# Shared up blocks inside the expert sweep, extra units between expert 61 and expert 62

## The reference

```python
scores = jax.nn.sigmoid(xs @ router_w)                 # 512 x 64
_, idx = lax.top_k(jnp.where(emask, sel, -jnp.inf), 6) # 6 experts of 64 per token
w = w / jnp.sum(w, axis=-1, keepdims=True) * 2.5
# every chosen (token, expert) pair: (silu(x @ w1[e]) * (x @ w3[e])) @ w2[e], width 256
routed = jax.ops.segment_sum(yg, slot_tok)             # summed per token with weight w
return routed + swiglu(xs, sh_w1, sh_w3, sh_w2)        # plus one shared expert, width 256
```

## Time and profile before

| | |
|---|---|
| median of three runs | 2140.44 us |
| profiled execution | 2133.77 us, of which the span is 2131.8 us |
| mean granted PE clock | 0.948 |
| PE busy | 1854.0 us (87%) |
| DVE busy | 859.0 us (40%) |
| ACT busy | 461.1 us (22%) |
| POOL busy | 373.6 us (18%) |
| SP's DMA queue | 499.70 MB, 58.3% of the time of the 16 engines |
| chain that ended last | PE 57%, DMA 19%, DVE 10%, issue 5%, POOL 5%, ACT 3% |

### The profile page before, as it was taken

How to read it: one execution, slowest core, us unless ns; L and a number is a source line. 1 busy time by engine, 2 the same in 40 slices (tenths; PEclk the granted TensorE clock), 3 DMA queues, 4 the chain that set the end, 5 groups by cost and what they waited for, 6 DMA issues and landing times.

```text
span 2131.8 us, 30544 instructions
## 1 busy us (share of the span) xinstructions
PE 1854.0 (87%) x9472; PEld 966.6 (45%) x9473; DVE 859.0 (40%) x1527; ACT 461.1 (22%) x823; POOL 373.6 (18%) x563
## 2 busy tenths in 40 slices
PE   5989999885999888788998899876889899989996
PEld 3455555333544444444444443344444444444543
DVE  1546666556322222222115499566222221212226
ACT  4134444212101011111110565220111111101112
POOL 0010000001111111111105288002111111111113
PEclk9999999996999999999999999887999999999997
DMA  9488010347999999999997202256999999999955
GB/s 405 176 340 330 1 40 20 139 173 304 357 420 393 402 400 394 401 404 396 383 382 262 123 1 119 79 227 269 399 406 402 399 387 408 402 400 396 398 182 211
DMA packets 95680, 625.10 MB, mean 293 GB/s; under 512 B 16128, under 2 KB 16256, under 8 KB 57472
## 3 DMA queue, kind: packets, MB, share of 16 engines
q1 hardware_dynamic: 44640, 499.70, 58.3%
q0 software_dynamic: 26112, 79.72, 10.3%
q10 hardware_dynamic: 24864, 44.84, 5.8%
HBM read 563.38 MB, written 76.28 MB: 300 GB/s over the span
## 4 chain that ended last, share of the span: by engine, by line
PE 57%; DMA 19%; DVE 10%; issue 5%; POOL 5%; ACT 3%; SPq 0%; POOLq 0%; DVEq 0%; ACTq 0%
DMA ring<-in 18%; PE PS L1064 12%; PE PS L1058 9%; PE PS L1071 6%; PE PS L1096 4%; PE PS L1085 4%; PE PS L1286 3%; PE PS L1049 3%; PE PS L986 3%; POOL work L581 3%; POOL work L613 3%; PE PS L1040 2%; PE PS L949 2%; PE PS L1004 2%; PE PS L1014 2%
## 5 line engine op out<-in xcount | busy, mean ns | idle before, releaser
L1064 PE MATMUL PS<-ring,work 128*64 128x256 f32 x3360 | 419.6, 406 | 112.8 <-issue 110.2
L1064 PEld LDWEIGHTS PS<-ring,work 128*64 128x64 f32 x3360 | 248.0, 146 | 260.5 <-issue 165.6
L1457 DVE TENSOR_TENSOR work<-work,PS 64x256 f32<-64x256 f32 x105 | 44.4, 423 | 521.9 <-ACT work L666 520.0
L1071 PE MATMUL PS<-ring,work 128*64 128x512 f32 x840 | 203.3, 605 | 1.0 <-DVE work L1469 1.0
L1058 PE MATMUL PS<-ring,work 128*128 128x512 f32 x400 | 184.3, 615 | 19.9 <-issue 8.6
L533 POOL COPY col_i<-idx 128x1 int32 (+1 forms) x128 | 23.4, 182 | 793.2 <-PE PS L1096 785.8
L1463 DVE COPY work<-PS 128x1024 f32<-128x1024 f32 x128 | 156.7, 1225 | 13.6 <-PE PS L1096 9.7
L539 POOL DMA_INDIRECT work<-h_rows,col_i x128 | 124.9, 976 | 165.2 <-issue 165.2
L666 ACT ACTIVATE work<-PS 64x256 f32<-64x256 f32 x105 | 39.5, 376 | 519.1 <-PE PS L1064 516.7
L1096 PE MATMUL PS<-cst,work 128*128 128x128 f32 x1040 | 142.4, 281 | 9.9 <-DMA work<-h_rows,col_i 9.9
L1096 PEld LDWEIGHTS PS<-cst,work 128*128 128x128 f32 x1040 | 115.0, 142 | 62.9 <-issue 52.8
(11 more groups left out here) (247 smaller groups left out, 2176.9 us busy)
## 6 DMA issues: line engine op xcount, KB each, us to landing
ring<-in SPq DMA_DIRECT2D x156, 2048.0 KB, 8.6
ring<-in SPq DMA_DIRECT2D x132, 1024.0 KB, 11.0
y_rows<-sq POOLq DMA_DIRECT2D x2, 14336.0 KB, 58.0
y_rows<-work ACTq DMA_DIRECT2D x210, 128.0 KB
ring<-in SPq DMA_DIRECT2D x3, 4096.0 KB, 15.4
y_rows<-work ACTq DMA_DIRECT2D x46, 256.0 KB
ring<-in SPq DMA_DIRECT2D x2, 3072.0 KB, 16.8
work<-in SPq DMA_DIRECT2D x2, 2048.0 KB, 17.4
```

What stands on the lines that cost most here:

```text
L1064: last = mm(bank(6)[64 * q:64 * q + 64, 0:F], lhs(c)[:, 0:64], w13(s)[:, q, c, :], start=(c == 0), stop=(c == DC - 1), tile_position=(0, 6 ...
L1071: last = mm(bank(4)[64 * q:64 * q + 64, :], actT[par][:, kk, 0:64], w2(s)[:, kk, q * 512:(q + 1) * 512], start=(kk == 0), stop=(kk == 1), ...
```

## The change

- The shared up weights go into `acc` (free between the row stores and the combine), at the start of SP's refills, with `sh_in`. Only the shared down weights still use a ring slot, now slot 2, after expert 61's down product.
- The loop over experts 3 to 62 becomes four loops (`PARTS`: experts 3 to 18, 19 to 30, 31 to 46, 47 to 58), on PE, DVE and ACT. After each PE makes one shared up block, and after the second and fourth ACT and DVE work it off. Experts 59 to 63 are written out.
- The extra units run between `unit(61)` and `unit(62)`. They have buffers of their own (`unit_x`, `unit_xT`, `unit_gate`, `unit_act`, `unit_actT`, `unit_y`), which lie in `acc` over the shared up weights, used up by then. Their weights go into slot 0.
- Expert 62 now uses slot 1 and expert 63 slot 3, so they follow experts 59 and 60 there. SP issues the extra unit's weights before theirs.
- Before expert 61's down product PE waits for expert 62's gate.
- The pointwise weights after layer 0 go out one expert earlier: the first DMA behind expert 61's down product, the second behind expert 62's.

```diff
+        shared_w13 = acc.rearrange("p t d -> p (t d)").rearrange("p (a c f) -> p a c f", a=2, c=DC)
+        unit_x, unit_xT, unit_y = acc[:, 0, :], acc[:, 1, :].rearrange("p (c t) -> p c t", c=DC), acc[:, 3, :]
+        unit_gate, unit_act, unit_actT = acc[:, 2, 0:F], acc[:, 2, F:2 * F], acc[:, 2, 2 * F:3 * F].rearrange("p (k t) -> p k t", k=2)
-        SHARED, EXTRA = 3, 2
+        SHARED, EXTRA = 2, 0
+        PARTS = ((0, 4), (4, 7), (7, 11), (11, 14))
         def slot_of(u):
-            return (3, 2, 0, 1)[u % RING]
+            return {E - 2: 1, E - 1: 3}[u] if u >= E - 2 else (3, 2, 0, 1)[u % RING]
...
# SP
+                sp.dma_start(acc.rearrange("p t d -> p (t d)"), sh_w[i][:, 0:UP]).then_inc(sh_in, 16)
                 refill_up(4, slot_of(4))
...
-                sp.wait_ge(m["up_ps"], E - 3)
-                sp.dma_start(slot_ap(SHARED)[:, 0:UP], sh_w[i][:, 0:UP]).then_inc(sh_in, 16)
-                refill_down(E - 1, slot_of(E - 1))
-                sp.wait_ge(m["dn_ps"], E - 3)
-                sp.dma_start(slot_ap(SHARED)[:, UP:SLOT], sh_w[i][:, UP:SLOT]).then_inc(sh_in, 16)
+                refill_up(E - 3, slot_of(E - 3))
+                refill_down(E - 4, slot_of(E - 4))
+                refill_down(E - 3, slot_of(E - 3))
                 sp.wait_ge(unit_rdy, i + 1)
-                sp.wait_ge(m["dn_ps"], E - 2)
+                sp.wait_ge(m["dn_ps"], E - 5)
...              (the loop over the extra units' weights)
+                sp.wait_ge(m["up_ps"], E - 4)
+                expert_up(ds(E - 2, 1), slot_of(E - 2), w_in[slot_of(E - 2)])
+                sp.wait_ge(m["dn_ps"], E - 4)
+                expert_down(ds(E - 2, 1), slot_of(E - 2), w_in[slot_of(E - 2)])
...              (the same for E - 1, one later)
+                sp.wait_ge(m["dn_ps"], E - 2)
+                sp.dma_start(slot_ap(SHARED)[:, UP:SLOT], sh_w[i][:, UP:SLOT]).then_inc(sh_in, 16)
...
+            load_pw1(0, 3)
             sp.wait_ge(M[0]["dn_ps"], E - 1)
-            load_pw1(0, 3)
-            sp.wait_ge(M[0]["dn_ps"], E)
             load_pw1(3, 6)
# PE
+                pe.wait_ge(sh_in, 16 + 32 * i)
+                for part, (g0, g1) in enumerate(PARTS):
+                    with nc.tensor.Fori(0, g1 - g0) as g:
+                        for r in range(4):
+                            unit(g * 4 + (4 * g0 + 3 + r), ...)
+                    if part == 2:
+                        pe.wait_ge(sh_gate, 1 + 2 * i)
+                    elif part == 3:
+                        pe.wait_ge(sh_act, 1 + 2 * i)
+                    shared_up(part // 2, part % 2)
+                for u in range(E - 5, E - 2):
+                    unit(u, slot_of(u), slot_of(u - 1), 32 * loads_of(u), 16 * ((u + 1) // 2 + 1), u % 2)
+                many = nc.tensor.value_load(unit_i[0:1, XMAX:XMAX + 1], min_val=0, max_val=XMAX)
+                with nc.tensor.If(many > 0):
+                    pe.wait_ge(xgT_ev, E - 1 + i * E)
+                    with nc.tensor.Fori(0, many) as j:
+                        ...      (the extra unit's four steps, with unit_x, unit_xT, unit_act, unit_actT)
+                unit(E - 2, ..., 0, E - 1 + i * E)      # with the wait for the gate
                 unit(E - 1, slot_of(E - 1), slot_of(E - 2), 32 * loads_of(E - 1), None, 1)
                 either(E - 1, lambda big: down(E - 1, 1, slot_of(E - 1), big))
# POOL: the extra unit's gather stands between those of expert 62 and expert 63
```

More of the change, by code:

```diff
@@ L549, in moe @@
                 gather(1, 1, xg_in[1])
-                with nc.gpsimd.Fori(0, E // 2 - 1) as g:
+                with nc.gpsimd.Fori(0, E // 2 - 2) as g:
                     for r in range(2):
@@ L705, in moe @@
                 either(1, lambda big: store(1, 0, 1, big))
[L706 to L713, removed]
                 def shared_silu(blk):
@@ L1172, in expert_in, with unit @@
                     pe.wait_ge(xgT_ev, u + 1 + i * E)
-                    pe.wait_ge(w_in[slot], n_w + i * 32 * LOADS)
+                    pe.wait_ge(w_in[slot], n_w + i * 32 * LOADS[slot])
                     either(u, lambda big: up(u, lambda c: xgT[par][:, c, :], slot, big))
-                def unit(u, slot, below, n_w, n_next, par):
+                def unit(u, slot, below, n_w, n_next, par, gates=None):
                     expert_in(u, slot, n_w, par)
@@ L1179, in unit @@
                         turn_rows(u + 1, n_next, 1 - par)
+                    if gates is not None:
+                        pe.wait_ge(gate_rdy, gates)
                     if below is not None:
@@ L1194, in moe, with shared_up @@
                 unit(2, slot_of(2), slot_of(1), 32, 32, 0)
-                with nc.tensor.Fori(0, (E - 4) // 4) as g:
-                    for r in range(4):
-                        unit(g * 4 + (3 + r), slot_of(3 + r), slot_of(2 + r), g * 32 + 32 * loads_of(3 + r),
-                             g * 32 + 16 * ((4 + r) // 2 + 1), (1 + r) % 2)
+                def shared_up(blk, a):
+                    for c in range(DC):
+                        last = mm(bank(3 * a), shared_w13[:, a, c, blk * 128:blk * 128 + 128], hM[:, c, :], start=(c == 0), stop=(c == DC - 1))
+                    last.then_inc(sh_ps, 1)
@@ new lines, in moe @@
+                pe.wait_ge(sh_in, 16 + 32 * i)
+                for part, (g0, g1) in enumerate(PARTS):
+                    with nc.tensor.Fori(0, g1 - g0) as g:
+                        for r in range(4):
+                            unit(g * 4 + (4 * g0 + 3 + r), slot_of(3 + r), slot_of(2 + r), g * 32 + (32 * g0 + 32 * loads_of(3 + r)),
+                                 g * 32 + (32 * g0 + 16 * ((4 + r) // 2 + 1)), (1 + r) % 2)
+                    if part == 2:
[3 more added lines that the diff above has]
+                    shared_up(part // 2, part % 2)
@@ L1200, in moe @@
+                unit(E - 2, slot_of(E - 2), slot_of(E - 3), 32 * loads_of(E - 2), 16 * ((E - 1) // 2 + 1), 0, E - 1 + i * E)
                 unit(E - 1, slot_of(E - 1), slot_of(E - 2), 32 * loads_of(E - 1), None, 1)
                 either(E - 1, lambda big: down(E - 1, 1, slot_of(E - 1), big))
-                def shared_up(blk, a):
-                    for c in range(DC):
-                        last = mm(bank(3 * a), w13(SHARED)[:, a, c, blk * 128:blk * 128 + 128], hM[:, c, :], start=(c == 0), stop=(c == DC - 1))
-                    last.then_inc(sh_ps, 1)
```

156 lines of the change are left out of this document (86 added, 70 removed).

## The result

The changed kernel takes 2159.16 us, the median of four runs (2157.22 to 2161.67), against 2140.07 us (2138.6 to 2141.09, also four runs) for the kernel before: ratio 1.0103, 95% interval 1.0087 to 1.0120, so 19.1 us slower. The forecast was 2155.4 us, slower.

The account below looks back on a forecast made before the run. Weight loads bound part of each sweep, PE its end. Terms summed to +8.7 us (layer 0) and +6.3 (layer 1), +15.0 together: 2148.8 us on the profiled execution, 2155.4 us as median, own range 2149 to 2162.

Parts of the forecast that it names:

- shared up weights at the start: Sweep start: 2 MB load slows first row gathers, 1.5 us (layer 0) and 3 (layer 1), upper bounds 2.5 and 4.7.
- blocks 1 to 3: After experts 18, 30, 46, mostly where loads lead: cost 0 in layer 0 (at most 1.5 us), 2 us in layer 1.
- block 4: After expert 58, where PE has no spare time: costs 7.1 us in layer 0, 6.6 in layer 1.
- extra unit: Between experts 61 and 62: 15.1 us serial chain plus 1.5 for count, branch and loop exit, 16.6 us per layer.
- end to first gather: Last down product to first combine gather: 26.3 us before, now 9.8 in layer 0 and 4.4 in layer 1.
- What bounds the kernel: Loads set the pace in some stretches of the sweep; at both sweeps' ends PE does, so work added there costs nearly full length.
- Rival A: Sweep's end: loads set the pace after all, fourth block and extra unit vanish there; 2108 us, faster, 7%.
- the sign that the prediction named for C: Behind expert 30: a DMA share below 1 in the following 20 us would show that loads run dry.
- rival C's first half: Loads run dry behind expert 30 in layer 1 (+5.1 us) and in layer 0 (+1.5); whole rival 2165 us, 15%.
- Rival D: Sweep's end: four loops and written-out experts cost PE idle time, 4.2 us per layer; 2164 us, 13%.
- the case in which it must wait for the loads: Layer 0's last store stuck until loads drain: gap of 12 us, sum 2.2 us higher.
- the rule quoted in the prediction: Layer 0's last store: DMA engines take turns between queues, so loads slow it but it need not wait until they drain.

Follow-up runs that it names:

- e10: Changed kernel with expert 63's result copied into a free piece of acc, not the buffer expert 61's store holds: 2157.87 us, 1.0098 to the kernel before.
- e3: Changed kernel with the four shared up blocks after experts 22, 26, 46 and 50, not 18, 30, 46 and 58: 2141.07 us, 1.0013 to the kernel before.
- e1: Changed kernel with the first two pointwise loads after layer 0 held until all expert stores have landed: 2160.07 us, 1.0108 to the kernel before.
- e5: Kernel before with only the shared up blocks moved, after experts 18, 30, 46 and 58; extra unit still behind expert 63: 2151.46 us, 1.0066.
- e4: Changed kernel with the shared blocks back behind the sweep under the gathers, so only the extra unit is moved: 2135.35 us, 0.9989 to the kernel before.
- e11: Kernel with only the extra unit moved, plus expert 63's result copied into a piece of acc: 2137.53 us, 1.0001 to the kernel before.
- e2: Changed kernel with the shared up weights issued behind the first refill, not ahead of it: 2155.09 us, 1.0079 to the kernel before.
- e7: Changed kernel with blocks after experts 22, 26, 46 and 50 and shared up weights behind the first refill: 2139.97 us, 1.0005 to the kernel before.
- e6: Kernel before with blocks after experts 22, 26, 46, 50, shared up weights behind the first refill, extra unit behind the sweep: 2137.75 us, 0.9995.

## Why the prediction was right, step by step

In the profiled pair, with e10 as a second execution of the same sweep; both in us.

| step | forecast L0 / L1 | changed kernel L0 / L1 | e10 L0 / L1 |
|---|---|---|---|
| shared up weights at the start | 1.5 / 3 | 2.9 / 6.5 | 1.4 / 6.7 |
| blocks 1 to 3 | 0 / 2 | 3.4 / 5.5 | -0.4 / 6.2 |
| block 4 | 7.1 / 6.6 | 6.9 / 6.4 | 6.9 / 6.4 |
| extra unit | 16.6 / 16.6 | 14.9 / 15.0 | 14.9 / 15.0 |
| end to first gather | 9.8 / 4.4 | 15.3 / 5.7 | 16.9 / 5.7 |

*What bounds the kernel:* right. Block 4 came out at full length in the stretch without spare time, 6.4 to 6.9 us each time; moved eight experts up (e3) it no longer did. Rival A (2108 us) is refuted by that and by the DMA share of 0.78.

*Blocks 1 to 3:* in layer 0 the size is open. e10, whose program is the same up to expert 63, shows -0.4 us, but e1 and e5, with the same three blocks, show 3.4 and 3.6, like the changed kernel, while e4 and e11, with no block there, show -0.4 and -0.2. Most executions thus speak for some 3.5 us, more than the forecast's 0 with its bound of 1.5. In layer 1 block 2, behind expert 30, keeps 4.6 us of its 6.9 (from +25.2 at expert 30 to +29.8 at expert 46). The loads did run dry behind it, the sign that the prediction named for C: DMA share 0.85 in the 20 us from the block on (the same 0.85 in e10; 1.00 before, 1.01 in e4), which is about 3 us without loads:

```profile
1765.90:1785.90 20.00, 20.00 (x110) 10.82 (x110) 3.60 (x6) 3.39 (x5) 1.32 (x3) 1.00 0.85 293
```

Behind block 2 of layer 0 the share is 0.99. This is rival C's first half in layer 1, in part: e4 and e11 lie 3.2 us above the kernel before between experts 18 and 58 of layer 1 without a block there, so of the 5.5 and 6.2 us in the table (4.2 in e1) some 1 to 3 are the blocks', about the 2 forecast.

*Extra unit:* the 15.1 us of the chain were right, and the 1.5 us for count, branch and loop exit were not needed. PE's row transposes of it begin at 1101.15 behind the activation transposes of expert 61 (1100.88), with no idle between them. Rival D (new code costs time) is refuted the same way: from expert 59 to 63 PE has no idle outside the extra unit but 0.5 and 0.6 us in front of expert 61's down product, where the new wait stands, and 0.5 us in front of the last down product, which stand there before as well, though the packets of instruction queue q8 rose from 38 to 59. The 0.82 and 1.16 us in front of expert 63 are gone.

*Start of the sweep:* the mechanism is right (e2), the size in layer 1 was not. The bound of 4.7 us counted only the gather's 5.7 us. Of the 6.5 us 4.3 stand at the first up product, where e2 took back 4.4; the rest comes up to expert 18, where e4, without these weights, shows 3.4 and e11 0.4, so it need not be theirs. PE's wait was longer and its clock lower: over the first up product the granted clock is 0.55, most of it at the 1.2 GHz level (0.66 before), and the same 32 matmuls take 6.60 us against 5.51:

```profile
1483.90:1490.50 6.60, 6.58 (x33) 3.56 (x33) 0.46 (x4) 0.00 (x0) 0.69 (x1) 0.55 0.05 14
```

The length of the wait alone does not set this: in layer 0 of e10 the same product took 5.01 us behind a wait of 8.34.

*End to first gather in layer 0* was the term most wrong, 9.8 forecast, 15.3 measured (16.9 in e10), beyond the upper bound of 12. The prediction priced a store sent into traffic by one row, 8.7 us, but that store went out 3.3 us ahead of the first pointwise load and not behind it; and it put the case in which it must wait for the loads at 12 us. e10, e4 and e11 show that this second case holds: the store lands only once the loads are through, some 23 us after the first pointwise load is sent. The 7.3 MB went out 8.7 us before the end, are through about 10 us behind it, and the store needs 4 us more. That its buffer was held by expert 61's store is true in the trace and explains nothing: e10 takes the wait away and wins nothing.

On the rule quoted in the prediction (engines take turns between queues, so the store is slowed and need not wait for the loads): these runs speak against drawing that from it. The same section of the Trainium skill, "DMA: Bandwidth & Descriptors", Queues, rings and completion order, also says that a semaphore increment is a strongly ordered write, which lands only after every earlier write of that DMA engine, across its queues. That was left out and points the way the runs went; no run here separates the data's arrival from the increment's, so it is not shown to be the cause.

*The sum:* +15.0 forecast; in the profiled pair +16.9 and +11.9, with 1.35 us from ahead of the layer-0 routing and -2.0 behind the last first gather +28.1. The medians say +19.1. The 9 us between are the 6.3 us by which the profiled execution before lies below its median and the 2.5 by which that of after lies above; every number of the table carries a part of them, such as the 3.2 us of layer 1 that e4 and e11 show too. Against the forecast, the terms were too small in the start of layer 1 (3.5), in the blocks (3.4 and 3.5) and above all in the gaps (5.5 and 1.3), and too large in the unit (1.7 and 1.6). The medians leave 4 us of this, and the traces cannot say how these 4 divide. So the direction and the main terms were right for the reasons given; that the sum came so near owes something to errors that cancel, above all the unit's against the gap's, and that part is luck.

**What stays open:** what the first three blocks cost in layer 0 (3.4 to 3.6 us in three traces, nothing in one), and the 3 to 5 us by which e3 and e7, with all blocks where loads lead, lie above e4 without them: their intervals overlap.

## What to carry to other kernels

Look for where an engine has idle time before filling it: moving three of four blocks by four to eight experts took back 18 us, and the busy time by stage told which. A piece of work taken out of a serial tail and put on the engine that sets the pace wins only the part that was not its own length: of the 26.3 us that went in layer 1, 15.0 came back as the extra unit's own chain and 5.7 as the gap behind the last expert. Such a piece can also cover a load: when e6 took a block of 7.1 us out of the tail, PE waited for the next weights instead. And price a small store that the next stage waits for by when the large loads ahead of it will be through, not by the store's own size.

## What the runs showed of the hardware

A 256 KB result store, sent as two DMAs of 128 KB, lands in 3.5 us in layer 1, where no loads ran, and in 14.6 us behind 7.3 MB of loads on another engine's queue (e10). Four loops in place of one and four more experts of written-out code cost PE no idle time that the trace shows, but for the half microsecond named above, though the instruction queue moved 59 packets in place of 38. The extra unit's up product took 7.1 us without a wait for its weights and 8.8 and 9.5 us behind such waits of 3.3 and 4.5 us, at granted clocks of 0.81 and 0.75. One program part executed twice (the sweep of layer 0 in the changed kernel and in e10) took 607.2 and 601.1 us, while that of layer 1 took 606.9 and 607.0: a single trace of before and after settles nothing below 6 us in 600.
